# Two-part activations as one 512-column stream in the square-ReLU layers, with the norm factor moved behind the second projection

## The reference, cut to what matters

```python
def rms_norm(x, g):
    y = x * lax.rsqrt(jnp.mean(x * x, axis=-1, keepdims=True) + EPS)
    return y * g

def squared_relu_mlp(h, w_up, w_down):
    a = jax.nn.relu(h @ w_up)          # 1024 -> 4096
    return (a * a) @ w_down            # 4096 -> 1024

# for each of the two layers i of the first block, after its attention:
h = rms_norm(x, mlp_norm[i])
x = x + squared_relu_mlp(h, mlp_w_up[i], mlp_w_down[i])
```

## Time and profile before

| what | value |
|---|---|
| runs | 1641.14, 1645.96 and 1647.43 us; median 1645.96 |
| the profiled execution: its span, first to last instruction | 1639.2 us |
| instructions | 31001 |
| PE busy | 1596.5 us, 97% of the span, 12665 matmuls |
| DVE busy | 1011.4 us, 62% |
| ACT busy | 763.7 us, 47% |
| granted TensorE clock over the span | 0.997 |
| DMA | 253.03 MB, mean 154 GB/s, queue 1 at 51.8% of 16 engines |
| up and down of layer 0 | about 163 to 253 and 253 to 342 us |
| up and down of layer 1 | about 451 to 541 and 541 to 630 us |

### The profile page before, as it was taken

One profiled execution on the slowest core, in us unless ns is written; L12 is line 12 of the kernel. 1 busy time (PEld: TensorE's weight loads), 2 busy tenths in 40 slices (PEclk: granted clock), 3 DMA queues, 4 the chain that ended last, 5 costly groups with the idle time before them and its releaser, 6 DMA issues.

```text
span 1639.2 us, 31001 instructions
## 1 busy us (share of the span) xinstructions
PE 1596.5 (97%) x12665; PEld 1522.2 (93%) x12665; DVE 1011.4 (62%) x1239; ACT 763.7 (47%) x1004; POOL 22.7 (1%) x40
## 2 busy tenths in 40 slices
PE   7989999998999999999999999999999999999999
PEld 5969999998999998999978999989999898889998
DVE  7786665567666546565457665466664656676653
ACT  4345554447555435434445444344443435654443
POOL 0000000013000000000000000000000000000000
PEclk9999999999999999999999999999999999999999
DMA  6701566644266665556622556635567352246673
GB/s 165 184 27 56 180 200 182 196 142 122 78 180 197 188 185 167 176 163 198 183 77 87 174 178 200 182 103 180 179 188 194 102 184 78 78 129 190 194 212 96
DMA packets 347111, 253.03 MB, mean 154 GB/s; under 512 B 32622, under 2 KB 345868, under 8 KB 347036
## 3 DMA queue, kind: packets, MB, share of 16 engines
q1 hardware_dynamic: 345424, 250.00, 51.8%
q10 hardware_dynamic: 1612, 1.97, 0.4%
HBM read 250.90 MB, written 1.05 MB: 154 GB/s over the span
## 4 chain that ended last, share of the span: by engine, by line
PE 86%; DVE 8%; ACT 3%; DMA 2%; issue 1%; SPq 0%; ACTq 0%; DVEq 0%
PE acc L537 25%; PE acc L539 25%; PE acc L538 25%; DVE w_low L1682 2%; ACT w_high L1194 1%; PE acc L562 1%; PE spare L735 1%; PE acc L767 1%; DMA w_raw<-in_ffn_w_dram 1%; PE spare L562 1%; PE acc L753 1%; DVE x_state L1892 1%; DVE xg_low L1726 1%; DVE evac_a L1890 1%; PE acc L1089 1%
## 5 line engine op out<-in xcount | busy, mean ns | idle before, releaser
L1682 DVE TENSOR_TENSOR w_low<-w_raw,w_high 128x2048 fp32r<-128x2048 f32 (+2 forms) x222 | 528.7, 2381 | 379.4 <-ACT w_high L1194 379.4
L1194 ACT ACTIVATE w_high<-w_raw 128x2048 fp32r<-128x2048 f32 (+2 forms) x222 | 441.4, 1988 | 612.9 <-PE acc L539 580.2
L537 PE MATMUL acc<-xg_high,w_high 128*128 128x272 f32 (+2 forms) x2320 | 663.3, 286 | 8.1 <-DVE xg_low L1726 4.4
L538 PE MATMUL acc<-xg_low,w_high 128*128 128x272 f32 (+2 forms) x2320 | 654.6, 282 | 0.0
L539 PE MATMUL acc<-xg_high,w_low 128*128 128x272 f32 (+2 forms) x2320 | 654.6, 282 | 0.0
L537 PEld LDWEIGHTS acc<-xg_high,w_high 128*128 128x128 f32 (+1 forms) x2320 | 435.4, 188 | 20.0 <-issue 9.3
L538 PEld LDWEIGHTS acc<-xg_low,w_high 128*128 128x128 f32 (+1 forms) x2320 | 435.4, 188 | 2.4 <-issue 1.7
L539 PEld LDWEIGHTS acc<-xg_high,w_low 128*128 128x128 f32 (+1 forms) x2320 | 435.4, 188 | 0.2
L537 PE MATMUL acc<-hidden_high,w_high 128*128 128x256 f32 (+1 forms) x1216 | 342.4, 282 | 2.8 <-DVE w_low L1682 2.8
L539 PE MATMUL acc<-hidden_high,w_low 128*128 128x256 f32 (+1 forms) x1216 | 341.7, 281 | 0.0
L538 PE MATMUL acc<-hidden_low,w_high 128*128 128x256 f32 (+1 forms) x1216 | 341.7, 281 | 0.0
(11 more groups left out here) (296 smaller groups left out, 1448.2 us busy)
## 6 DMA issues: line engine op xcount, KB each, us to landing
w_raw<-in_ffn_w_dram SPq DMA_DIRECT2D x88, 1024.0 KB, 5.3
w_raw<-in_ffn_w_dram SPq DMA_DIRECT2D x32, 1408.0 KB, 7.0
w_raw<-in_mlp_w_up_dram SPq DMA_DIRECT2D x32, 1024.0 KB, 5.7
w_raw<-in_mlp_w_down_dram SPq DMA_DIRECT2D x32, 1024.0 KB, 5.6
w_raw<-in_attn_w_qkv_dram SPq DMA_DIRECT2D x12, 1024.0 KB, 5.1
w_raw<-in_a_w_in_dram SPq DMA_DIRECT2D x18, 256.0 KB, 4.3
w_raw<-in_a_w_in_dram SPq DMA_DIRECT2D x4, 1024.0 KB, 8.0
w_raw<-in_a_w_out_dram SPq DMA_DIRECT2D x4, 1024.0 KB, 5.1
```

What stands on the lines that cost most here:

```text
L537: pe.matmul(dst, high_w, high, start=first, stop=False)
L538: pe.matmul(dst, high_w, low, start=False, stop=False)
L1194: act.activation(whi[slot(c)][:, 0:SIZES[c]], raw[c % 2][:, 0:SIZES[c]], ACT.Copy).then_inc(S["w_high"], 1)
L1682: dve.tensor_tensor(wlo[slot(c)][:, s], raw[c % 2][:, s], whi[slot(c)][:, s].bitcast(F32), ALU.subtract)\
```

## The change

`xg_high` and `xg_low` become the two halves of one tile `xg_parts`, and `hidden_high` and `hidden_low` of one tile `hidden_parts`, at the same places as before. In the square-ReLU layers alone a triple becomes a pair (`both`): the high weight tile with high and low activations as one stream of 512 columns (two stretches of 256) into a whole PSUM bank of 512 columns, and the low weight tile with the high activations into the bank's first 256 columns. The two halves of a bank are added later. In up, ScalarE copies the second halves to `evac_a` ahead of its split, VectorE adds the first halves, and a further VectorE operation makes max(s, 0) times s, which replaces ScalarE's square. No norm factor is applied there. In down VectorE multiplies both halves by the squared factor and adds them to `x_state` in two operations, each waiting for the one before. The sums of squares, the root and the refining move from around units 0 and 1 to after unit 1 (TensorE's part from unit 1 to unit 2), and one more operation squares the factor.

```diff
-        XH = place("xg_high", [P, KD, ROW], F32R)
-        XL = place("xg_low", [P, KD, ROW], F32R)
+        XB = place("xg_parts", [P, 2, KD, ROW], F32R)
+        XH, XL = XB[:, 0], XB[:, 1]
...
-        HH = place("hidden_high", [P, HID], F32R)
-        HL = place("hidden_low", [P, HID], F32R)
+        HB = place("hidden_parts", [P, 2, HID], F32R)
+        HH, HL = HB[:, 0], HB[:, 1]
...
+            def both(bank, high_w, low_w, parts, first, last):
+
+                pe.matmul(bank, high_w, parts, start=first, stop=False)
+                return pe.matmul(bank[:, 0:SEQ], low_w, parts[:, 0], start=False, stop=last)
...
+                        if joined:
+                            ins = both(acc[u % 2][:, m, :], *w, XB[:, :, k, 0:SEQ], k == 0, k == KD - 1)
...
+                            if joined:
+                                ins = both(acc[u % 2][:, 0, :], *w, HB[:, :, h:h + SEQ], first, last)
...
-                wide(g, 1, T0, T, between=norm_sum)
+                wide(g, 1, T0, T, joined=joined)
                 for j in range(2, 4):
-                    wide(g, j, T0, T)
+                    wide(g, j, T0, T, between=norm_sum if j == 2 else None, joined=joined)
...
+                    par = j % 2
+                    sem_, value = unit_full(g, j)
+                    act.wait_ge(sem_, at(value, it, 2))
+                    act.activation(ta[par][:, :, 0:SEQ], acc[(g.u0 + j) % 2][:, :, SEQ:], ACT.Copy)\
+                        .then_inc(S["low_copied"], 1)
                     if not last:
                         split(g.c0 + j + 2, it, 2)
-                    par = j % 2
-                    act.wait_ge(S["dve_evac"], at(g.r0 + j + 1, it, 2))
-                    act.activation(tb[par][:, :, 0:SEQ], ta[par][:, :, 0:SEQ], ACT.Square).then_inc(S["act_step"], 1)
-                    act.wait_ge(S["act_step"], at(step0 + j + 1, it, 2))
+                    act.wait_ge(S["mid_made"], at(mid0 + j + 1, it, 2))
...
-                root(SEQ)
-                step0 = n.get("act_step")
+                mid0 = n.get("mid_made")
                 unit(0)
                 unit(1)
+                root(SEQ)
...
-                    unit_wait(g, j, it, 2)
-                    dve.scalar_tensor_tensor(ta[par][:, :, 0:SEQ], acc[(g.u0 + j) % 2][:, :, 0:SEQ], 0.0,
-                                             across(rstd[:, 0:SEQ], 2), ALU.max, ALU.mult).then_inc(S["dve_evac"], 1)
+                    s = ta[par][:, :, 0:SEQ]
+                    dve.wait_ge(S["low_copied"], at(lc0 + j + 1, it, 2))
+                    dve.tensor_tensor(s, s, acc[(g.u0 + j) % 2][:, :, 0:SEQ], ALU.add).then_inc(S["dve_evac"], 1)
+                    dve.wait_ge(S["dve_evac"], at(g.r0 + j + 1, it, 2))
+                    dve.scalar_tensor_tensor(tb[par][:, :, 0:SEQ], s, 0.0, s, ALU.max, ALU.mult)\
+                        .then_inc(S["mid_made"], 1)
...
+                unit(0)
+                unit(1)
                 variance(SEQ)
                 refine(rstd, SEQ)
-                unit(0)
-                unit(1)
+                link(dve.tensor_tensor(rstd[:, 0:SEQ], rstd[:, 0:SEQ], rstd[:, 0:SEQ], ALU.mult))
...
-                    dve.tensor_tensor(tile(X), tile(X), acc[(g.u0 + j) % 2][:, 0:1, 0:SEQ], ALU.add)\
-                        .then_inc(S["dve_evac"], 1)
+                    parts = ta[j % 2][:, :, 0:SEQ]
+                    dve.tensor_tensor(parts, acc[(g.u0 + j) % 2][:, 0].rearrange("p (a t) -> p a t", a=2),
+                                      across(rstd[:, 0:SEQ], 2), ALU.mult).then_inc(S["down_scaled"], 1)
+                    dve.wait_ge(S["down_scaled"], at(ds0 + 2 * j + 1, it, 4))
+                    dve.tensor_tensor(tile(X), tile(X), parts[:, 0:1], ALU.add).then_inc(S["down_scaled"], 1)
+                    dve.wait_ge(S["down_scaled"], at(ds0 + 2 * j + 2, it, 4))
+                    dve.tensor_tensor(tile(X), tile(X), parts[:, 1:2], ALU.add).then_inc(S["dve_evac"], 1)
```

More of the change, by code:

```diff
@@ L385, in two_blocks_kernel @@
             xg_ready sq_made sq_read norm_sum log_made guess_made dve_step act_step hid_high hid_ready
-            gate_silu rope_turned kr_ready kr_spread q_raw rope_done q_spread k_low angle_ready half_ready lam_ready lam_exp v_turned tables_ready hide_ready
+            gate_silu low_copied mid_made down_scaled rope_turned kr_ready kr_spread q_raw rope_done q_spread k_low angle_ready half_ready lam_ready lam_exp v_turned tables_ready hide_ready
             v_ready wi_in wi_turned wi_ready idx_full idx_relu idx_read s_full s_read exp_done probs_ready
@@ L566, in short, with wide @@
                 pe.matmul(sp[0][:, 1, 0:SHORT], tiles[:, 0:P], tiles[:, 0:SHORT], start=True, stop=True)
-            def wide(g, j, T0, T, ready=None, it=None, per=0, tiles=None, between=None, beside=None, high=XH, low=XL):
+            def wide(g, j, T0, T, ready=None, it=None, per=0, tiles=None, between=None, beside=None, high=XH, low=XL,
+                     joined=False):
                 c, u = g.c0 + j, g.u0 + j
@@ L580, in wide @@
                             w, rows_ = tiles(c, k, m)
-                        ins = three(acc[u % 2][0:rows_, m, 0:T], *w, high[:, k, 0:T], low[:, k, 0:T],
-                                    k == 0, k == KD - 1)
+                        if joined:
+                            ins = both(acc[u % 2][:, m, :], *w, XB[:, :, k, 0:SEQ], k == 0, k == KD - 1)
+                        else:
+                            ins = three(acc[u % 2][0:rows_, m, 0:T], *w, high[:, k, 0:T], low[:, k, 0:T],
+                                        k == 0, k == KD - 1)
                         if between is not None and k == 0 and m == 0:
@@ L627, in turn_rope, with down @@
                           start=True, stop=True).then_inc(S["rope_turned"], 1)
-            def down(g, T, K, chunks):
+            def down(g, T, K, chunks, joined=False):
                 kc = K // chunks
@@ L644, in unit @@
                                 pe.wait_ge(S["hid_ready"], n.get("hid_ready"))
-                            ins = three(acc[u % 2][:, 0, 0:T], *cols(c, k * P, (k + 1) * P), HH[:, h:h + T],
-                                        HL[:, h:h + T], q == 0 and k == 0, q == chunks - 1 and k == kc - 1)
+                            first, last = q == 0 and k == 0, q == chunks - 1 and k == kc - 1
+                            w = cols(c, k * P, (k + 1) * P)
+                            if joined:
+                                ins = both(acc[u % 2][:, 0, :], *w, HB[:, :, h:h + SEQ], first, last)
+                            else:
+                                ins = three(acc[u % 2][:, 0, 0:T], *w, HH[:, h:h + T], HL[:, h:h + T], first, last)
                         ins.then_inc(S["w_used"], 1)
@@ L667, in sum_residual, with up @@
                     .then_inc(S["norm_sum"], 1)
-            def up(g, T0, T, groups, outputs, idle, norm_sum=None, but=0):
+            def up(g, T0, T, groups, outputs, idle, norm_sum=None, but=0, joined=False):
                 begin(g, but)
                 keep_busy(sp[0][:, 0], idle)
-                wide(g, 0, T0, T, xg_waits(groups), beside=None if norm_sum else sum_tiles(T))
+                wide(g, 0, T0, T, xg_waits(groups), beside=None if norm_sum else sum_tiles(T),
+                     joined=joined)
                 if norm_sum is None:
@@ L683, in up @@
                     for j in range(4, 6):
-                        wide(g, j, T0, T, it=i, per=2)
+                        wide(g, j, T0, T, it=i, per=2, joined=joined)
                 n.add("hid_ready", outputs)
             def mlp(layer):
-                up(G[f"mlp_up{layer}"], META, SEQ, PAIRS, KF // 2, 0, sum_residual, 1)
-                down(G[f"mlp_down{layer}"], SEQ, KF, 2)
+                up(G[f"mlp_up{layer}"], META, SEQ, PAIRS, KF // 2, 0, sum_residual, 1, True)
+                down(G[f"mlp_down{layer}"], SEQ, KF, 2, True)
             def ffn(i, T0, T):
@@ L1267, in mlp @@
                     unit(j)
-                n.add("act_step", g.units)
+                n.add("mid_made", g.units)
                 g = G[f"mlp_down{layer}"]
@@ L1835, in unit @@
                         split(g.c0 + j + 2)
-                hh0 = n.get("hid_high")
+                hh0, lc0 = n.get("hid_high"), n.get("low_copied")
+                unit(0)
+                unit(1)
                 variance(SEQ)
                 refine(rstd, SEQ)
-                unit(0)
-                unit(1)
+                link(dve.tensor_tensor(rstd[:, 0:SEQ], rstd[:, 0:SEQ], rstd[:, 0:SEQ], ALU.mult))
                 with dve.Fori(0, g.units // 2 - 2) as i:
@@ L1847, in mlp @@
                 n.add("hid_high", g.units)
+                n.add("low_copied", g.units)
                 g = G[f"mlp_down{layer}"]
-                sq0, xh0, sm0 = n.get("squares"), n.get("xg_high"), n.get("sq_made")
+                sq0, xh0, sm0, ds0 = n.get("squares"), n.get("xg_high"), n.get("sq_made"), n.get("down_scaled")
                 def down_unit(j, it=None):
```

(1 more changed line is left out.)

## The result

| | before | after |
|---|---|---|
| median of six runs, us | 1641.0 (1639.6 to 1647.4) | 1656.9 (1653.4 to 1660.7) |
| profiled span, us | 1639.2 | 1657.3 |
| matmuls | 12665 | 11641 |
| granted clock over the span | 0.997 | 0.992 |

The ratio after to before is 1.0079, 95% interval 1.0058 to 1.0100: slower by about 13 us (the medians lie 15.9 apart).

A forecast was written before the change was run, and what follows sets the result against it. TensorE's three split-product matmuls were taken as the bound. Layer 0 at +1.0 and layer 1 at -0.7 us gave +0.3 on the 1639.2 span, with about 7 around it: 1646.3 us, range 1636 to 1660.

The forecast's parts named there:

- rival 3: In up and down, the pair falls into a slow pace, 354 ns instead of 340; about +17 us, 1663; chance 0.13.
- the prediction's own sign: The prediction is wrong if the pair is outside 324 to 340 ns or TensorE waits at every unit of up.
- Part 1, the stream: In up and down, the pair takes 333.3 ns, gaining 6.7; 0.107 us per up unit, 0.214 per down unit.
- a per-column cost: A rival in up and down: the 6.7 ns is per column, the pair gains 0; +5.4 us, 1651.4; chance 0.16.
- Part 2, the chain beside up: In steady up, ScalarE's 0.59 us copy of the low half ahead of the split is hidden by 0.14 us.
- Part 3, start of up: Units 0 and 1 no longer need the norm factor: 0.5 us gone per layer, no wait for unit 4's split.
- the fixed terms: Terms beside the pair's pace; for the start of up, -0.5 us per layer.
- Part 4, up to down: From up to down the last chunk is split later, so TensorE resumes 0.8 us later: +0.8 per layer.
- Part 5, down: In down x_state is ready 1.20 us later; waits of 0.72 (layer 0) and 0.18 (layer 1); +1.2 at each end.
- The sum: Over the changed layers: layer 0 +1.0 us, layer 1 -0.7, together +0.3.

The follow-up runs named there:

- e4: The kernel before without the 64-column matmul in first and second projections; triple at 340 ns, in down of layer 1 at 353 ns.
- e6 to e12: Changed kernel with activations, weights or up's low half moved (pair 347 to 353 ns), or both weight tiles on 512 columns (467); kernel before, weights moved (triple 360).
- e5: The norm factor's move alone, with the triples of the kernel before and no 512-column stream; 0.999 of before (0.9973 to 1.0008).
- e1: Changed kernel with the 512-column stream issued as two 256-column matmuls, except each unit's first product; 1.0095 of before (1.0062 to 1.0127).

## Why the prediction was right and wrong

The range 1636 to 1660 held 1656.9, and that was luck: it ended on the near side of rival 3, which was meant to lie outside it, and the kernel came in below it because the kernel before is 5 us faster over six runs than over the three that I started from, and because rival 3's sum was 2.4 us too high. The forecast itself, 1646.3 and no change, did not come true; rival 3 did, with the chance of 0.13 that I gave it. By the prediction's own sign, a pair outside 324 to 340 ns, it was wrong.

**Part 1, the stream: the step that failed.** I took the 6.7 ns on top of each 256 columns for a cost per instruction and put the pair at 333.3 ns. It takes 353.3: 20 ns x 1024 = 20.5 us of error, and rival 3 had this number (354) from the earlier trace rows. The evidence that I put against a per-column cost was the earlier trace rows, ten matmuls of 512 columns with 2 ns on top. But those take two passes over their columns, and the moving tile is read at half the pace; they say nothing on a one-pass stream. And I called the pace of the layers "the layer's own" without asking what keeps it. The earlier trace rows side by side, one instruction with two paces in one kernel, were the warning: the pace depended on something that the change alters. e4 shows that the faster one can hang on one small matmul, e6 to e12 that the pace hangs on the place of the tiles; the layout of before was the good one for a triple of 256 columns and is not for the pair. My argument against rival 3, that in these layers the fast pace holds for tens of units, was an argument about the triple, and not quite true of it: the trace of before has 48 triples at 353 ns in one of these layers, from 547 to 564 us.

The rule of the Trainium skill that I set beside it ("TensorE: Matmul & The Clock Gate", Back-to-back issue gap) would give 325 ns for the pair; the section calls that formula the gap of an isolated matmul. The trace has 353, 28 ns more, and the lowest pace of the pair in any run is 347.

**Part 2, the chain beside up: right.** The copy out of PSUM takes 0.60 (0.59 expected), moves the split by 0.50, and TensorE waits for w_low nowhere in steady up.

**Part 3, start of up: right.** No wait at unit 2, none at unit 4 (its split is whole at 185.70, 186.3 expected). Per layer, up without the pace's 3.4 us is 0.8 shorter than before, where the fixed terms were -0.5; alone (e5) the factor's move gives -0.36.

**Part 4, up to down: right within 0.25.** The boundary is 254.06, TensorE goes on at 261.15: 7.09 after it against 6.41 in the earlier trace rows. +0.7 for the +0.8 expected; in layer 1 it is 6.97, +0.6.

**Part 5, down: the chain right, its price gone with the slower pace.** From the multiplication to the second add's end it is 1.74 us against 0.42, +1.3 for +1.2. I had the supply ready 11.39 after the boundary. With the pair at 353 ns a unit takes 11.31, so the waits of 0.72 shrink to the 0.08 that is left: the trace has 0.10 (301.12). A slower TensorE hid the longer chain. Where a unit of e1 runs at 340, the wait is there: 11.37 after the boundary for 11.39. At the end, 1.70 for 0.51 idle: +1.2, as expected.

**The sum.** In the changed layers: 13.0 from the pace, two ends of down 2.4, two starts of the second half 0.8 (beside their pace), the short waits in down of layer 0 0.5, starts of up -1.6; together 15.1, for the 15.0 that the traces show. Rival 3's terms add up to 17.5: pace 13.6 (it took all 1024 triples at 340), ends 2.4, starts of the second half 1.6 (in part because it counted the slower pace of the first half unit twice), waits 0.9, starts of up -1.0. The whole times give 13 (9.5 to 16.4), which holds the 15.

**What stays open.** Why a distance between moving and weight tiles costs 20 to 40 ns per 768 columns is not shown; a collision of the two reads in SBUF would fit e6 to e12, and is only argued. Why the pair has no pace of 340 where the triple has one is open with it: it was never seen faster than 347, and no run has the 512-column streams without the copies and the writes to the bank's second half. Whether the opening 512-column product or the writes to the second half hold e1 in the slow pace was not separated. The other halves and distances (the low half of down, the two weight tiles against each other) were not tried, so a placement at which the pair runs at 340 or less isn't excluded.

## What to carry to other kernels

Price a stream of matmuls by the starts of that very instruction, one-pass or two-pass, on those tiles, and where a trace holds two paces of one instruction, take the slower as a case with real weight and ask what keeps the faster. Fewer instructions and weight loads need not bring anything; here 1024 of each went, the columns stayed, and the kernel got slower. And of a chain beside the bound engine that is made longer, the price is the excess over that engine's new time, so work both out together.

## What the runs showed of the hardware that I had not expected

At 2.4 GHz, 768 columns of one-pass float32r matmuls with 128x128 weight loads between them took 340 to 360 ns, by where the moving tile lay against the weight tile modulo 256 bytes: the triple 340 or 353 at 64 and 360 with the weights moved by 192, the pair 353 at 64, 351 at 0, 347 or 353 at 128 and 349 or 353 at 192. 320 is the columns alone. At one placement there can be two paces: 340 and 353 for the triple (one 64-column matmul ended the slower one, and the faster then held for 65 us), 347 and 353 for the pair. Two stretches 36 KB apart in one stream cost the same as one contiguous stretch (353 both).
